# Vector gathers issued four rows behind the input gathers, and semaphore clears moved into the row stage

## What is computed

```python
best, pos = lax.top_k(cand, PEER_TOPK)                 # 16 experts for each of 8 heads
experts = jnp.take_along_axis(cand_ix, pos, axis=-1)
gates = jax.nn.softmax(best, axis=-1).astype(h.dtype)
...
act = jax.nn.gelu(jnp.einsum('nd,nhkd->nhk', tb, peer_u[eb]))
return jnp.einsum('nhk,nhkd->nd', gb * act, peer_v[eb])
```

## Time and profile before

| What | Value |
|---|---|
| median of three runs | 5552.89 us (5552.31 to 5563.88) |
| time of the profiled execution | 5552.56 us |
| its span, first to last instruction | 5550.8 us |
| busy: PE, DVE, ACT, POOL | 4455.3, 3357.7, 1393.2, 2866.8 us |
| granted TensorE clock, mean | 0.925 |
| transfers | 1471.60 MB, of them 1342.34 MB by the gathers |

### The profile page before, as it was taken

How to read it: one execution, slowest core, us unless ns; L and a number is a source line. 1 busy time by engine, 2 the same in 40 slices (tenths; PEclk the granted TensorE clock), 3 DMA queues, 4 the chain that set the end, 5 groups by cost and what they waited for, 6 DMA issues and landing times. The chain is left out here.

```text
span 5550.8 us, 51217 instructions
## 1 busy us (share of the span) xinstructions
PE 4455.3 (80%) x15092; PEld 2373.3 (43%) x15092; DVE 3357.7 (60%) x8542; ACT 1393.2 (25%) x3530; POOL 2866.8 (52%) x2690
## 2 busy tenths in 40 slices
PE   8788898687878778777697888978878787787775
PEld 3588664333333333332245886644333333333322
DVE  5555474666666666666455554746666666666664
ACT  1211452222222222222202114522222222222221
POOL 0032000777777777777500220007777777777775
PEclk9888899999999999999898888989999999999998
DMA  6100002999999999999760000039999999999997
GB/s 241 38 3 1 15 1 83 388 379 390 385 388 384 384 381 372 389 391 390 306 241 8 3 1 15 1 113 396 373 375 391 388 384 379 379 378 384 398 391 295
DMA packets 425564, 1471.60 MB, mean 265 GB/s; under 512 B 46529, under 2 KB 52289, under 8 KB 424769
## 3 DMA queue, kind: packets, MB, share of 16 engines
q0 software_dynamic: 368640, 1342.34, 62.8%
q1 hardware_dynamic: 56640, 125.89, 6.4%
HBM read 1464.49 MB, written 3.57 MB: 264 GB/s over the span
## 5 line engine op out<-in xcount | busy, mean ns | idle before, releaser
L1519 PE MATMUL psall<-ring,diag 128*128 128x512 f32 x5120 | 2490.1, 638 | 808.5 <-ACT diag L1408 808.2
L1331 DVE CUSTOM_DVE_ANT_0 ring<-ring,mixed 128x1024 f32<-128x1024 f32 x1280 | 1565.9, 1223 | 1158.6 <-DMA ring<-in_peer_u,eidx 1157.5
L1519 PEld LDWEIGHTS psall<-ring,diag 128*128 128x128 f32 x5120 | 1005.0, 203 | 2252.2 <-issue 2250.4
L1253 POOL DMA_INDIRECT ring<-in_peer_u,eidx x1280 | 1285.2, 1004 | 1138.0 <-DVE eidx L1193 748.4
L1253 POOL DMA_INDIRECT ring<-in_peer_v,eidx x1280 | 1404.9, 1098 | 457.8 <-issue 324.3
L1416 ACT ACTIVATE act<-dot 128x2 f32<-128x2 f32 x640 | 130.1, 203 | 2482.0 <-DVE dot L1331 2482.0
L1408 ACT ACTIVATE diag<-cons,wgt 128x128 f32<-128x128 f32 x1280 | 443.0, 393 | 209.2 <-DVE wgt L1311 206.4
L463 POOL TENSOR_TENSOR mlt<-lt,lmask 128x512 f32<-128x512 f32 x120 | 174.6, 1465 | 474.4 <-DVE lt L549 336.5
L1475 PE MATMUL psall<-h2T,wq 128*128 128x128 f32 (+1 forms) x1024 | 285.5, 434 | 1.3 <-DVE x L1293 1.3
L455 POOL MEMSET state<- 64x512 f32 x2 | 1.0, 518 | 513.8 <-POOLq L374 513.8
L1475 PEld LDWEIGHTS psall<-h2T,wq 128*128 128x128 f32 x1024 | 157.3, 191 | 132.3 <-issue 130.5
(11 more groups left out here) (285 smaller groups left out, 4854.3 us busy)
## 6 DMA issues: line engine op xcount, KB each, us to landing
mixed<-in_w_mod SPq DMA_DIRECT2D x32, 1024.0 KB, 5.3
wq<-in_w_pq SPq DMA_DIRECT2D x64, 512.0 KB, 6.6
ring<-in_peer_u,eidx POOLq DMA_INDIRECT x1280, 6.5
ring<-in_peer_v,eidx POOLq DMA_INDIRECT x1280, 6.5
wring<-in_w_mod SPq DMA_DIRECT2D x8, 2048.0 KB, 14.5
wring<-in_w_in_tm SPq DMA_DIRECT2D x4, 2048.0 KB, 12.7
ring<-in_w_out SPq DMA_DIRECT2D x4, 2048.0 KB, 11.4
wring<-in_w_in_fm SPq DMA_DIRECT2D x2, 2048.0 KB, 8.2
```

Of the source, the lines that this page charges most:

```text
L1253: nc.gpsimd.indirect_dma_start(out=ring[:, n % slots, :], out_offset=None, in_=d[table], in_offset=bass.IndirectOffsetOnAxis(ap=p.eidx[:, ...
L1331: nc.vector.tensor_tensor_reduce(out=p.u[:, n % UR, :], in0=p.u[:, n % UR, :], in1=p.mixed[:, t, :], scale=1.0, scalar=0.0, op0=ALU.mult, ...
L1519: mm = nc.tensor.matmul(bank, p.diag[:, n % VR, :], p.v[:, n % VR, 512 * c:512 * c + 512], start=(s == 0), stop=(s == UNIT - 1))
```

## The change

Two things change. The vector gathers are issued four rows behind the input gathers: u0 to u3 first, then u4, v0, u5, v1 and so on, and at the end u639, v635, v636, v637, v638, v639. All waits in front of the gathers keep their meaning, and the rings keep 8 slots each. And the semaphores of the front stages are cleared by SP inside the block of `tail`, behind its last `wq` load; at the end of the layer only those are cleared that `tail` itself made.

```diff
+LAG = 4
...
                 sp.dma_start(p.wq[:, i % WR, :, :], d["w_pq"][bass.ds(lay, 1), i % (4 * C)].rearrange("l p k n -> p (l k) n")
                              ).then_inc(sem(f"load_q{i % WR}"), 16)
+            for name in p.front_sems:
+                sp.sem_clear(sem(name))
...
-            for n in range(ROWS):
-                if n % TOPK == 0:
-                    pool.wait_ge(sem("routed"), n // TOPK + 1)
-                if n >= UR:
-                    pool.wait_ge(sem("dots"), n - UR + 1)
-                gather(p.u, UR, "peer_u", "u_in", n)
-                if n >= VR:
-                    pool.wait_ge(sem("row_free"), n - VR + 1)
-                gather(p.v, VR, "peer_v", "v_in", n)
+            for n in range(ROWS + LAG):
+                if n < ROWS:
+                    if n % TOPK == 0:
+                        pool.wait_ge(sem("routed"), n // TOPK + 1)
+                    if n >= UR:
+                        pool.wait_ge(sem("dots"), n - UR + 1)
+                    gather(p.u, UR, "peer_u", "u_in", n)
+                m = n - LAG
+                if m >= 0:
+                    if m >= VR:
+                        pool.wait_ge(sem("row_free"), m - VR + 1)
+                    gather(p.v, VR, "peer_v", "v_in", m)
...
-        outer = set(p.sems)
+        p.outer = set(p.sems)
...
-            for name, s in p.sems.items():
-                if name not in outer:
-                    nc.sync.sem_clear(s)
+            for name in p.tail_sems:
+                nc.sync.sem_clear(p.sem(name))
...
-            tail(p, lay)
+            p.front_sems = sorted(set(p.sems) - p.outer - set(p.delta_sems))
+            p.tail_sems = p.names_of(tail, lay)
```

## The result

The changed kernel takes 5400.6 us (median of four runs, 5387.9 to 5405.5) against 5552.6 us for the kernel before on the same chip: a ratio of 0.972, interval 0.970 to 0.974, some 152 us faster. The forecast was 5481 with a range of 5425 to 5534.

A forecast was written before the change was run, and what follows sets the result against it. GpSimd's continuous gather issue was taken to bound the row stage, with the DMA engines nearly the bound. Row stage 50, its end 9 and clears 12 sum to 71 us: 5552.6 to 5481 us, range 5425 to 5534.

The forecast's parts named there:

- The wait for row_free: Row stage: GpSimd's 66 us wait for vector slots nearly all goes with the four-row delay, gaining 50 us.
- the bound of 115: Row stage, upper end: every stretch runs like three with little waiting, 115 us less in both layers.
- the fourth rival: Row stage: more gathers are held by dots and the kernel is slower, 5681 us; chance 0.07.
- The third rival: Row stage: the transfer backlog never runs dry, every stretch at 409 GB/s, 5325 us; chance 0.10 for this or half.
- The first two rivals: Row stage gains nothing, as transfers bound it or the slot wait stays; about 5532 us, chance 0.18 together.
- The first: Row stage: transfers are the bound, only end and clears gain, 5532 us; chance 0.18 together with the second.
- The end of the stage: End of each row stage: the last dot comes earlier and the last vectors meet ready weights, 9 us in both layers.
- The clears: Layer-end barrier: 107 semaphore clears a layer move behind SP's last `wq` load and are covered, 12 us.

The follow-up runs named there:

- The square of four times: Dot or one-input sum in its place, each without and with the four-row delay, all with moved clears: 5545.1 and 5400.6 us; 5403.9 and 5363.9 us.
- dot_psum_lag4: Changed kernel with the dot's second input read from two PSUM banks, filled by ScalarE, and one bank each for projections and scores: 5375.7 us, ratio 0.968.
- sum_lag0: Changed kernel with the old gather order, moved clears kept, and a one-input sum in place of the dot: 5403.9 us, one run.
- smallwq_lag4: Changed kernel with the 20 `wq` loads inside the row stage bringing one of eight chunks: 5428.6 us, ratio 0.977.
- lag4_slots4: Changed kernel, but a vector gather may start only four rows ahead instead of eight: 5602.2 us, ratio 1.008.
- lag0_u5_v10: Changed kernel with the old gather order, five input and ten vector slots, eight diagonals kept: 5452.5 us, ratio 0.979.

## Why the forecast was wrong

**The wait for row_free: right in what it counted.** The forecast took 50 of the 66 us of visible wait; 45 went from GpSimd's waits, though what they brought in time was not measured apart. The reason given, that a vector lies unused in its slot, bears out. What ended the idle time before TensorE's row matmul (us, times), before and after:

```profile
  ACT diag L1408: 808.2, 404
...
  DMA ring<-in_peer_v,eidx: 2028.4, 1891
  ACT diag L1414: 116.2, 75
```

TensorE now waits for landings, and hardly for a diagonal.

**The step that failed** is the one that made this the whole of the row stage. The stage gained 138 us, outside even the bound of 115. The sum had found that gathers lose four times as much by being held as by waiting, 280 us, and then gave the 280 no term. The ground for it stands against the fourth rival: "a dot follows the landing of its own u, and u and v still alternate, so nothing shifts the two against each other". They do shift: the vector gathers that start in the first 0.75 us of a dot fell from 17 to 7 in a hundred, at an unchanged price of some 1.6 us each, and the loss by holds fell by 91 us, to 189. The square of four times shows that this counts: with no holds to lose, the same change is worth 40 us and not 144. The upper bound failed with it, since it was taken from stretches of a kernel whose median landing was 6.5 us.

**The third rival, "the queue stays full",** was given 0.10 for all of it or half; the stage's 138 us are two thirds of its 207. Its mechanism is what the first 600 us of layer 0's stage show: 408 to 409 GB/s and median landings of 12.7 to 13.9 us. It fails late in both stages, as the backlog is used up: landings at 6.6 us in 2300 to 2500, 383 GB/s in 4940 to 5140. Its weak point was that it spoke of "no interruptions" and not of the reach and the `wq` loads, which decide it.

**The first two rivals and the fourth** are excluded by the stage's time. The first, that the transfers are the bound, comes true only in `dot_psum_lag4`. The fourth's mechanism worked in reverse: the mean gather went from 1.05 to 2598.7 / 2560 = 1.015 us. (Its price is 148 us and not 149; nothing hangs on that.)

**The end of the stage: right,** 9 us forecast, 8.4 measured. **The clears: right,** 12 forecast, 12.6 by VectorE's idle time at the boundary, though 51 a layer moved and not 107: the rest went away altogether, which the sum missed without harm.

**What stays open.** That a longer reach lowers the time lost to holds is shown, and that fewer gathers then start early in a dot. With a backlog a hold is also covered, as transfers wait in the queue anyway: 1400 to 1600 has a mean gather of 1.01 us and still 408 GB/s. Why the starts shift is not shown. They do so where no backlog forms as well, in the pair with small `wq` loads (22 to 15%), but less than in the changed kernel. A ring of 16 vector slots in the old order, the plainest test of the reach, was not tried.

## What to carry to other kernels

When an in-order engine issues transfers, work out for each wait on its queue how many transfers may be in flight behind it: an order that puts a wait on an older event lets the engine run further ahead. Here this shifted where its transfers were issued, so that fewer were held, and where other loads pushed the landings back it let a backlog form that covered stalls. Don't treat time lost inside instructions as fixed because it isn't listed as waiting; if it is four times the visible wait, it deserves its own range and its own rival. And look for whether the collision itself can be removed: here moving one operand to PSUM was worth some 25 us more.

## What the runs showed of the hardware

- A gather that starts inside a VectorE pass with one input in SBUF, or with its second input in PSUM, takes 0.94 us (means of 943 to 949 ns in `sum_lag0` and `dot_psum_lag4`). Started in the first 0.75 us of a dot with two inputs in SBUF it takes 1.58 us in the mean in the kernel before, and up to 1.98. The Trainium skill, "SBUF — State Buffer", section Who interferes with whom, says that a VectorE instruction with at most one SBUF input, outside the 2-port modes, does not contend with GpSimd; these 943 to 949 ns agree.
- The gathers hold 408 to 409 GB/s for hundreds of microseconds, and fewer bytes need not make a kernel faster: `smallwq_lag4` has 45 us fewer transfers and gains nothing on the changed kernel.
- TensorE's granted clock is 1.00, its level of 2.4 GHz, in the five stretches of the changed kernel above, where it was 0.92 to 0.95 before. It does not make the gain by itself: `lag4_slots4` has 0.98 to 1.00 and is slower than the kernel before, and `lag0_u5_v10` gains some 100 us at 0.93 to 0.97. Whether it has a part in the step from 11 to 13 rows, where it rises to 1.00, is not shown.
